# A fused three-layer transformer kernel: the first differential residual behind the last projections, a wait of TensorE's start moved, and the softmax scaling of two attentions on GpSimd

## The reference

```python
# forgetting attention, and in the same form latent attention
p = jax.nn.softmax(logits, axis=-1)
outs.append(jnp.einsum('bhqk,bhkd->bhqd', p, vf[:, :, :q1]))
...
# differential attention: two maps for each of 8 heads
p = masked_softmax(sc, chunk_mask(blk, s)[None, None, None])
a = p[:, :, 0] - lam * p[:, :, 1]
return jnp.einsum('bhqk,bkhe->bqhe', a.astype(v.dtype), v)
...
o = rms_norm(o, subln_g) * (1.0 - lambda_init)
return o.reshape(b, s, D_MODEL) @ w_o      # added to x: the residual
```

## Time and profile before

| | us |
|---|---|
| median of 3 runs | 1846.24 (1845.83 to 1846.66) |
| the profiled execution | 1846.94 |
| its span, first to last instruction | 1845.1 |
| mean granted clock of TensorE | 0.996 of full speed |

### The profile page before, as it was taken

How to read it: one execution, slowest core, us unless ns; L and a number is a source line. 1 busy time by engine, 2 the same in 40 slices (tenths; PEclk the granted TensorE clock), 3 DMA queues, 4 the chain that set the end, 5 groups by cost and what they waited for, 6 DMA issues and landing times.

```text
span 1845.1 us, 23148 instructions
## 1 busy us (share of the span) xinstructions
PE 1822.6 (99%) x8960; PEld 1514.5 (82%) x8960; DVE 1127.0 (61%) x1906; ACT 804.0 (44%) x1434; POOL 145.4 (8%) x149
## 2 busy tenths in 40 slices
PE   9999999999999999998999999999999999999998
PEld 7898788888887988887888888879888888888887
DVE  4577644344345777685663663664989776366375
ACT  6562432222235555554442432446766544144244
POOL 4003200000004100002000000023100010000000
PEclk9999999999999999998999999999999999999999
DMA  5212322332233211112233322322011122233232
GB/s 157 71 36 67 102 91 92 100 94 92 91 96 98 69 56 60 58 58 69 92 92 98 96 92 92 94 85 80 26 47 46 58 91 92 92 94 100 91 111 73
DMA packets 128251, 152.17 MB, mean 82 GB/s; under 512 B 9291, under 2 KB 100973, under 8 KB 128141
## 3 DMA queue, kind: packets, MB, share of 16 engines
q1 hardware_dynamic: 127980, 150.62, 26.3%
q10 hardware_dynamic: 160, 0.07, 0.1%
HBM read 148.50 MB, written 2.10 MB: 82 GB/s over the span
## 4 chain that ended last, share of the span: by engine, by line
PE 93%; DVE 3%; issue 1%; ACT 1%; POOL 1%; DMA 0%; DVEq 0%; POOLq 0%; ACTq 0%
PE bk L1648 22%; PE bk L1650 22%; PE bk L1649 22%; PE bk L1677 5%; PE bk L1679 5%; PE bk L1678 5%; PE bk L1653 4%; PE bk L1736 1%; PE bk L1738 1%; PE bk L1737 1%; PE bk L1715 1%; PE bk L1722 1%; DVE XT L1799 1%; PE bk L1742 1%; POOL FS L2108 1%
## 5 line engine op out<-in xcount | busy, mean ns | idle before, releaser
L1648 PE MATMUL bk<-R,WH 128*128 128x512 f32 x1764 | 701.8, 398 | 4.0 <-DVE R L1793 2.8
L1649 PE MATMUL bk<-R,WH 128*128 128x512 f32 x1764 | 697.5, 395 | 0.0
L1650 PE MATMUL bk<-R,WL 128*128 128x512 f32 x1764 | 697.4, 395 | 0.0
L1787 DVE TENSOR_TENSOR WL<-RAW,WH 128x1024 fp32r<-128x1024 f32 (+4 forms) x277 | 341.8, 1234 | 533.2 <-ACT WH L1968 532.2
L1968 ACT ACTIVATE WH<-RAW 128x1024 fp32r<-128x1024 f32 (+4 forms) x277 | 288.0, 1040 | 650.6 <-PE bk L1650 591.0
L1648 PEld LDWEIGHTS bk<-R,WH 128*128 128x128 f32 x1764 | 331.3, 188 | 83.6 <-issue 5.1
L1650 PEld LDWEIGHTS bk<-R,WL 128*128 128x128 f32 x1764 | 331.2, 188 | 81.1
L1649 PEld LDWEIGHTS bk<-R,WH 128*128 128x128 f32 x1764 | 331.5, 188 | 78.5
L1677 PE MATMUL bk<-WH,R 128*128 128x512 f32 (+4 forms) x528 | 186.2, 353 | 0.0
L1678 PE MATMUL bk<-WH,R 128*128 128x512 f32 (+4 forms) x528 | 180.1, 341 | 0.0
L1679 PE MATMUL bk<-WL,R 128*128 128x512 f32 (+4 forms) x528 | 180.1, 341 | 0.0
(11 more groups left out here) (149 smaller groups left out, 1765.6 us busy)
## 6 DMA issues: line engine op xcount, KB each, us to landing
RAW<-in_ffn_w_up_dram SPq DMA_DIRECT2D x176, 256.0 KB, 3.0
RAW<-in_ffn_w_down_dram SPq DMA_DIRECT2D x44, 512.0 KB, 3.7
RAW<-in_w_gate_dram SPq DMA_DIRECT2D x44, 256.0 KB, 2.9
RAW<-in_w_up_dram SPq DMA_DIRECT2D x44, 256.0 KB, 3.1
RAW<-in_w_down_dram SPq DMA_DIRECT2D x22, 512.0 KB, 3.6
RAW<-in_da_w_qkv_dram SPq DMA_DIRECT2D x32, 256.0 KB, 2.9
RAW<-in_w_out_dram SPq DMA_DIRECT2D x8, 512.0 KB, 3.6
RAW<-in_da_w_qkv_dram SPq DMA_DIRECT2D x8, 512.0 KB, 3.5
```

Source lines behind the costliest of these rows:

```text
L1648: e.matmul(dst, lh, rh, start=start, stop=False)
L1649: e.matmul(dst, lh, rl, start=False, stop=False)
L1650: return e.matmul(dst, ll, rh, start=False, stop=stop)
L1787: e.tensor_tensor(low, RAW[:, r, 0:m], high.bitcast(F32), ALU.subtract).then_inc(on["wlo_dve"], 1)
```

## The change

It does three things.

1. The residual of group 0 of the differential attention goes from between the K and V projections of group 2 to behind the projections of group 3, ahead of the residuals of groups 1 and 2; its two weight blocks move with it.
2. `tensor_program` waits for the identity (`s_id`) ahead of the first step that PE has part in and that isn't `warm`. Before, it waited ahead of the first step of any engine that was neither `warm` nor `gemm_f`, which is the first of all.
3. In forgetting and latent attention `p_one` is cut in two: DVE makes the reciprocal (`p_root`), GpSimd the multiplication (`p_one`), and `turn` waits for GpSimd. The planner assumes 200 ns + 1.0 ns per column for it.

```diff
-    "p_one": {"dve": 2}, "p_two": {"dve": 4}, "turn": {"pe": 1}, "value": {"pe": 1},
+    "p_root": {"dve": 1}, "p_one": {"pool": 1}, "p_two": {"dve": 4}, "turn": {"pe": 1}, "value": {"pe": 1},
...
-        if kind == "p_one":
-            return 190.0 + 230 + 0.54 * width_of(f["p"])
...
+    if kind == "p_one":
+        return 200.0 + 1.0 * width_of(f["p"])
     if kind == "rope":
...
         for g in range(4):
             plan_qk(qkv, g, 0, 1024)
-            if g == 2:
-                plan_rows(da_o, 0, 2)
             plan_v(qkv, g, 2048, 0)
-        for g in (1, 2):
+        for g in (0, 1, 2):
             plan_rows(da_o, g * 256, 2)
...
                 if maps == 1:
-                    st = yield step("p_one", z=z, rz=rz, p=p1, after=L.p_done)
+                    st = yield step("p_root", z=z, rz=rz, after=L.p_done)
+                    shared = (yield step("p_one", rz=rz, p=p1, after=[st.dve])).pool
                 else:
...
                     fsl.put(L.p[1], st.dve)
+                    shared = st.dve
...
-                st = yield step("turn", bank=b.i, src=FS[:, L.p[0].i, 0:nk], i=i, odd=odd, after=counts([b.free, st.dve]))
+                st = yield step("turn", bank=b.i, src=FS[:, L.p[0].i, 0:nk], i=i, odd=odd, after=counts([b.free, shared]))
...
-            if between:
-                yield from between
             yield from gemm_t(N.X, 8, 264 if extra else 256, ev_v)
...
-                yield from qkv_group(Gs[g], g, ND, "da", g == 3, prior, before, first_part() if g == 2 else None)
-            for g in (1, 2):
+                yield from qkv_group(Gs[g], g, ND, "da", g == 3, prior, before)
+            for g in (0, 1, 2):
                 yield from till(Gs[g])
                 yield from residual(Gs[g].O, 2)
...
-                if k not in ("warm", "gemm_f"):
+                if k != "warm" and "pe" in SIGNALS[k]:
                     w.wait_ge(s_id, 16)
...
-                elif k == "p_one":
-                    for done in st.after:
-                        w.wait_ge(*done)
-                    e.reciprocal(st.rz, st.z).then_inc(on["p_one_dve"], 1)
-                    w.wait_ge(on["p_one_dve"], st.dve0 + 1)
-                    e.tensor_scalar(st.p, st.p, st.rz, None, ALU.mult).then_inc(on["p_one_dve"], 1)
+                elif k == "p_root":
+                    for done in st.after:
+                        w.wait_ge(*done)
+                    e.reciprocal(st.rz, st.z).then_inc(on["p_root_dve"], 1)
...
+                elif k == "p_one":
+                    for done in st.after:
+                        w.wait_ge(*done)
+                    e.tensor_scalar(st.p, st.p, st.rz, None, ALU.mult).then_inc(on["p_one_pool"], 1)
```

More of the change, by code:

```diff
@@ L191, in takes @@
                 "root_out": 760.0, "both_in": 370.0, "both_out": 370.0, "eighth": 170.0, "lam_in": 500.0, "lam": 500.0,
-                "gate_in": 400.0, "gate_log": 190.0, "out_in": 160.0, "kv_mean": 170.0, "q_root": 170.0, "fg_cols": 160.0}.get(kind, 690.0)
+                "gate_in": 400.0, "gate_log": 190.0, "out_in": 160.0, "kv_mean": 170.0, "q_root": 170.0, "fg_cols": 160.0, "p_root": 190.0}.get(kind, 690.0)
+    if kind == "p_one":
+        return 200.0 + 1.0 * width_of(f["p"])
     if kind == "rope":
@@ L1026, in in_line, with qkv_group @@
                 spawn(fill_by(t, pairs), 0)
-        def qkv_group(G, g, N, kind, spent, prior=None, before=None, between=None):
+        def qkv_group(G, g, N, kind, spent, prior=None, before=None):
             new_group(G, 2)
@@ L1501, in products @@
             yield from ffn(N4, value_conv(1), None)
-        def first_part():
-            yield from till(Gs[0])
-            yield from residual(Gs[0].O, 2)
         def way_out(O):
```

## The result

The changed kernel takes **1851.42 us** (median of 9 runs, 1849.87 to 1852.04), against 1846.66 for the kernel before on the same chips (9 runs, 1845.47 to 1848.23). The ratio is **1.0023, 95% interval 1.0013 to 1.0034**: slower, where 9.5 us less were forecast. The profiled execution took 1850.16 us, its span 1848.4, at a mean granted clock of 0.999. Lines of the code have moved by 6 to 8: `wlo` is now L1781, transposes are L1647, `sums` L1709, `lo` L1787, the GpSimd sum L2100, and GpSimd's multiplication by 1/z is L2104.

A forecast was written before the change was run, and what follows sets the result against it. TensorE, busy 1822.6 of 1845.1 us, was taken as the bound, so only its waits and lower clock could be gained. Terms -8.1 - 1.4 + 0 = -9.5 us from the median 1846.2 gave 1836.7 us, range 1832.5 to 1842.5.

The forecast's parts named there:

- the 11 us of filler: Between group 2's K and V projections: attention has 11 us less filler after the residual moves; forecast cost 0.
- the clock's share of 3.4 us: End of differential attention: half of 6.8 us busy at the lower clock, 3.4 us, goes with the waits.
- The step up to the first projection: Program start: x lands at 9.3 us, four transposes follow, first projection at about 9.8 instead of 11.14.
- 1.4 us sooner: Program start: first projection 1.4 us sooner, taken as -1.4 us for the whole, ends 0 and -2.8.
- rival E: Program start: early TensorE start brings nothing or delays the clock's rise; 1838 to 1840, inside the 0.66 shared with the forecast.
- the nearest: GpSimd's multiplication priced by the one-input cast, 1.19 us for 1024 columns: 0.65 us at 512, about 0.45 mean.
- If one in ten has none: Transposes in forgetting and latent attention start 0.2 us later; one in ten without room costs 1.9 us against 1.6 gained.
- rival C: Forgetting and latent attention: longer exp-to-transpose path exposed nearly every time, slower than before, decisive from 0.10 us each; chance 0.08.
- Rival B: GpSimd's multiplication costs as much as its two-input sum; some transposes wait, +3 to +5 us, 1840 to 1842; chance 0.12.
- Rival D: Forgetting and latent attention: waits from GpSimd and DVE excluding each other at SBUF dominate, all 6 us exposed, 1843; chance 0.06.
- Relief of DVE: Forgetting and latent attention: DVE loses 40 us of work; PE's 1.6 us of waits for crowded DVE can be gained.
- The range: Whole kernel: from 1832.5 us (13.6 us gained) to 1842.5, where the rival of the two-input sum's price ends.

The follow-up runs named there:

- e16: Kernel before plus residual move and later identity wait, 1/z on DVE, plan's GpSimd sum price raised for the second residual alone: 1837.19 us, 0.9951.
- e17: Kernel before plus the residual move alone, with the plan's GpSimd sum price raised for the second residual alone: 1837.13 us, 0.9951.
- e12: Changed kernel with a GpSimd copy of the tile onto itself in place of the multiplication by 1/z: 1841.45 us, 0.9975 of the kernel before.
- e1: Kernel before plus residual move and later identity wait, multiplication by 1/z left on DVE: 1838.76 us, 0.9959.
- e5: Changed kernel with the multiplication's measured price in the plan and more units ahead (4 and 6 for 2 and 4): 1838.30 us, 0.9953.
- e18: Changed kernel with measured multiplication price, more units ahead, and GpSimd sum price raised for the second residual alone: 1837.26 us, 0.9951.
- e13: Kernel before plus residual move and later identity wait, 1/z on DVE, plan's price of every GpSimd sum raised to 1.70 us: 1839.73 us, 0.9965.

## Why the prediction was wrong

**Part one was right.** -8.1 us were forecast; the differential part took 8.6 less, the kernel with this part alone 8.8 less. The waits for `diag` and `lo` are gone, the 11 us of filler that were taken from group 2 were not missed, and the clock's share of 3.4 us was measured as 3.2.

**Part two was too large.** -1.4 us were forecast, with 0 as the upper end, and it is 0. The step up to the first projection was nearly right: x landed at 9.8 instead of 9.3, so the projection came at 10.22 instead of 9.8, 0.9 us sooner than before and not 1.4. The step "1.4 us sooner" was then carried to the end of the program without looking at what else depends on when things happen. Five runs against five (e16 and e17) show nothing at the end, and with the new start the clock mostly falls 0.6 ms later. That is rival E as to the time. Where the gain goes with the clock at 1.00 is seen in part. In e16 PE starts at 1.31 us and in e17 at 3.55, but the first projections come at 10.26 and 10.54: in e16 the eight transposes and four `warm` products ahead took 1.91 and 2.06 us, in the changed kernel 1.03 and 1.17, and why they took twice as long no row tells. The first sums follow at 32.1 and 32.6 us, and 0.4 us is within the spread from one execution to another (31.4 to 32.9 in 14 traces with the new start, 32.0 to 34.0 in 6 with the old).

**Part three failed, and it decides the sign.** The sum has it at 0, and it is +12.7. The failed step is the choice of the row for the price. The prediction had three rows and took the cast, "the nearest", with one input, for an instruction that does arithmetic. The multiplication has the price of the two-input sum, 1.57 us at 512 columns, 2.4 times the assumed one. e12 is the proof from the other side: with an instruction of the assumed price in its place the kernel takes 1841.45, inside the range. The second failed step is the exposure. "If one in ten has none" and 0.2 us each gave 1.9 us; the number of visible waits was about right (14 of 96, 5.4 us), but the cost was 12.7 us, 0.13 us for each of the 96, past the 0.10 that rival C names as the point from which it decides. The evidence used was the earlier trace rows, PE's one wait in 96 in the kernel before. It says how often the path was late with a multiplication of 0.42 us; it says nothing about the slack behind it. Rival B, the price of the sum, was put at +3 to +5 us by "a few tenths at some transposes"; with that price it was the mechanism of C.

How the 12.7 us stand in the trace can be told nearly in full. Windows over the latent part, of the changed kernel and of e1:

```profile
1229.00:1488.00 259.00, 249.72 (x1455) 215.66 (x1454) 164.03 (x343) 154.27 (x367) 108.51 (x109) 1.00 0.16 50
```

```profile
1227.00:1476.00 249.00, 245.64 (x1454) 216.07 (x1453) 186.35 (x407) 153.42 (x367) 37.90 (x45) 1.00 0.17 52
```

PE is idle for 9.3 us in the one and 3.4 in the other, 5.9 of the 9.9 us. The rest lies within PE's busy time, whose modelled ends hide short waits; it shows when one goes by starts. Take the step from the start of the matmul before to the start of a transpose of FS that waits for a semaphore. In the forgetting part these steps sum to 7.7 us in the changed kernel and to 4.6 in e1, which is the whole 3.1; in the latent part to 19.3 and 12.4, which is 6.9 of the 9.9, and 12.6 in e12. Most of the other 3 us are the waits between 1305 and 1331 us that e12 has too.

**Rival D** was no matter: in 1300 to 1450 us the mean `wlo` of 1024 columns rose from 1.22 to 1.27 us, over 9 of them, 0.5 us in all. The exclusion that the earlier trace rows show, which the Trainium skill states ("SBUF — State Buffer", Who interferes with whom), was met too seldom to be where the time went. **Relief of DVE** brought nothing: e1 and e5 are 0.5 us apart, e16 and e18 0.1.

**The signs.** Of the signs that the prediction had named, the clock at 1.00 in every stretch, the waits near 840 and PE's first matmul came true; GpSimd's multiplications (0.60 to 2.02 us instead of 0.25 to 0.65) and PE's waits for them (5.4 us instead of under 3) did not.

**The range** missed because the upper end took the dear price with the cheap exposure. Both bounds together, the price of the sum and 0.1 to 0.2 us each at 96 places, would have reached from 1846 to 1856.

## What to carry to other kernels

Take the price of an instruction from a row of the same operation on the same engine: on GpSimd a copy, a cast or a memset says nothing about a multiplication. Where no such row exists, the dear end goes together with its exposure, since a path with one visible wait in 96 may have no slack for more. An order that is fixed ahead must be made with the measured durations, and a longer link in a chain also needs more units under way; with both, an instruction 2.7 times as long (1.11 us in the mean against 0.41 on DVE) cost nothing. And a short wait of TensorE beside small products can cost several times its length through the clock, in some executions and not in others: look at the granted clock there before the times of two versions are compared.

## What the hardware showed unexpectedly

GpSimd multiplies a 128-row float32 tile by a column in 0.64, 0.92, 1.29 and 1.57 us for 128, 256, 384 and 512 columns (by a constant in 1.50 us at 512), but copies it in 0.33, 0.40, 0.51 and 0.63 us. ScalarE multiplies 512 columns by a column in 0.72 us. And a wait of 0.4 us with 16 one-column products behind it let TensorE's clock fall in 8 of 10 profiled executions with the new start and in none of 4 with the old, 1.5 to 1.8 us each time, and in none of 6 (e13 to e18) in which six products of 512 columns stood ahead of those products and the wait was gone. Why a start that comes 2 us sooner changes this 590 us later was not found.
